# First block: high and low parts made from x times norm weight behind each residual sum, token norms applied to the products, embedding projection inside the FFN

## What is computed

```python
def rmsnorm(x, g):
    return x * lax.rsqrt(jnp.mean(x * x, axis=-1, keepdims=True) + EPS) * g

def first_block(...):
    h = x
    for i in range(2):
        hn = rmsnorm(h, norm_mix_g[i])
        if i == 0:  h = h + conv_dsa_mixer(hn, ...)        # stage "even"
        else:       h = h + gated_deltanet_mixer(hn, ...)  # stage "odd"
        # stage ffn0 / ffn1
        h = h + swiglu(rmsnorm(h, norm_ffn_g[i]), w_gate, w_up, w_down)
        # stage ple0 / ple1
        e = rmsnorm(p[i] @ ple_w_proj[i], ple_post_norm_g[i])
        h = h + e * jax.nn.sigmoid(rmsnorm(h, ple_norm_g[i]) @ ple_w_gate[i])
    return h
```

## Time and profile before

| | us |
|---|---|
| median of 3 runs (2429.23 to 2435.3) | 2432.1 |
| the profiled execution, whole | 2434.55 |
| its span, first to last instruction | 2433.2 |
| PE busy | 1919.7 (79%) |
| PE weight loads | 1371.9 (56%) |
| DVE busy | 949.6 (39%) |
| ACT busy | 709.6 (29%) |

### The profile page before, as it was taken

One profiled execution on the slowest core, in us unless ns is written; L12 is line 12 of the kernel. 1 busy time (PEld: TensorE's weight loads), 2 busy tenths in 40 slices (PEclk: granted clock), 3 DMA queues, 4 the chain that ended last, 5 costly groups with the idle time before them and its releaser, 6 DMA issues.

```text
span 2433.2 us, 30159 instructions
## 1 busy us (share of the span) xinstructions
PE 1919.7 (79%) x13222; PEld 1371.9 (56%) x13222; DVE 949.6 (39%) x1719; ACT 709.6 (29%) x1157; POOL 4.1 (0%) x11
## 2 busy tenths in 40 slices
PE   6788997788898998769877888978868765655656
PEld 4687997678776998637654333424246632322323
DVE  6765555666556554544463010101064520100001
ACT  4444444563524444334441000000034410000000
POOL 0000000000000000000000000000000000000000
PEclk9899998999999999889988999999988978888787
DMA  6234453331167545461042999999942369999997
GB/s 234 96 136 167 157 184 133 147 139 70 70 243 274 194 155 197 191 256 74 1 173 116 428 427 429 428 428 427 428 167 104 139 270 427 427 428 427 427 428 327
DMA packets 44787, 606.53 MB, mean 249 GB/s; under 512 B 5104, under 2 KB 5232, under 8 KB 6768
## 3 DMA queue, kind: packets, MB, share of 16 engines
q1 hardware_dynamic: 43488, 597.61, 60.8%
q0 software_dynamic: 880, 4.98, 0.6%
q10 hardware_dynamic: 288, 2.02, 0.2%
HBM read 603.54 MB, written 1.05 MB: 248 GB/s over the span
## 4 chain that ended last, share of the span: by engine, by line
PE 50%; DMA 28%; DVE 14%; ACT 6%; issue 2%; SPq 0%; DVEq 0%; POOLq 0%; ACTq 0%
PE ps L85 48%; DMA m_last_slot<-moe_down 15%; DMA m_more<-moe_up 9%; DVE m_WL L94 2%; PE ps L88 2%; ACT m_WH L91 1%; DMA m_ring<-ada 1%; ACT m_mix_sc L91 1%; DVE m_od L100 1%; DVE m_misc L103 1%; DVE m_wk L100 1%; DVE m_misc L112 1%; ACT m_od L91 1%; DVE m_wk L94 1%; DMA m_praw<-pT 1%
## 5 line engine op out<-in xcount | busy, mean ns | idle before, releaser
L85 PE MATMUL ps<-m_ring,m_moe_sc 128*32 128x256 f32 (+1 forms) x2304 | 414.8, 542 | 82.0 <-DMA m_ring<-moe_gate 76.9
L94 DVE TENSOR_TENSOR m_WL<-m_ring,m_WH 128x1024 fp32r<-128x1024 f32 (+1 forms) x277 | 331.8, 1203 | 310.7 <-ACT m_WH L91 310.3
L91 ACT ACTIVATE m_WH<-m_ring 128x1024 fp32r<-128x1024 f32 (+1 forms) x277 | 285.0, 1036 | 159.9 <-PE ps L85 153.1
L85 PE MATMUL ps<-m_nH,m_WH 128*128 128x256 f32 x1136 | 291.2, 292 | 14.9 <-ACT m_WH L91 14.8
L85 PE MATMUL ps<-m_nL,m_WH 128*128 128x256 f32 x1136 | 288.0, 289 | 3.0 <-DVE m_nL L94 3.0
L85 PEld LDWEIGHTS ps<-m_ring,m_moe_sc 128*32 128x32 f32 (+1 forms) x2304 | 155.8, 142 | 228.6 <-issue 115.9
L85 PE MATMUL ps<-m_more,m_moe_sc 128*32 128x256 f32 (+1 forms) x768 | 210.2, 562 | 85.3 <-DMA m_more<-moe_up 85.3
L85 PEld LDWEIGHTS ps<-m_nH,m_WH 128*128 128x128 f32 x1136 | 224.1, 197 | 20.9 <-ACT m_WH L91 17.3
L94 DVE TENSOR_TENSOR m_nT<-ps,m_nT 128x512 f32<-128x512 f32 (+1 forms) x32 | 17.9, 558 | 555.9 <-PE ps L85 555.9
L85 PEld LDWEIGHTS ps<-m_nL,m_WH 128*128 128x128 f32 x1136 | 224.0, 197 | 5.4 <-DVE m_nL L94 5.0
L91 ACT ACTIVATE m_nT<-ps 128x512 f32<-128x512 f32 (+1 forms) x64 | 31.4, 491 | 620.2 <-PE ps L88 327.2
(11 more groups left out here) (268 smaller groups left out, 2808.4 us busy)
## 6 DMA issues: line engine op xcount, KB each, us to landing
m_ring<-moe_gate SPq DMA_DIRECT2D x64, 2048.0 KB, 19.2
m_ring<-moe_up SPq DMA_DIRECT2D x32, 2048.0 KB, 17.7
m_more<-moe_up SPq DMA_DIRECT2D x32, 2048.0 KB, 22.2
m_more<-moe_down SPq DMA_DIRECT2D x32, 2048.0 KB, 18.0
m_last_slot<-moe_down SPq DMA_DIRECT2D x32, 2048.0 KB, 22.5
m_ring<-ada SPq DMA_DIRECT2D x24, 2048.0 KB, 8.2
m_ring<-ffn_down SPq DMA_DIRECT2D x16, 1408.0 KB, 6.1
m_ring<-ffn_gate SPq DMA_DIRECT2D x10, 2048.0 KB, 8.1
```

Of the source, the lines that this page charges most:

```text
L85: return Issued() if self.dry else self.e.matmul(out, lhsT, rhs, start=start, stop=stop, skip_group_check=skip)
L91: return Issued() if self.dry else self.e.activation(*a, **k)
L94: return Issued() if self.dry else self.e.tensor_tensor(*a)
```

## The change

- Parts of x: the next stage's high part is made by ACT as x times norm weight (a `[128,1]` scale of the activation) behind each residual sum, before that sum's square; the low part by DVE in one operation (x times weight minus high). No `rr` goes into them. `following(tag)` names the next stage. For odd they lie in new tiles `oddH`, `oddL`, and the tiles of odd are moved for it.
- The token norm `rr` is applied to products: DVE multiplies each gate tile pair by `rr` from PSUM to SBUF, and ACT takes Silu or Sigmoid there. `up` isn't scaled; the `down` sums are multiplied by `rr` before they are added to x. In even and odd, products with tokens on the partitions are scaled by ACT with `r_tok`, the others by DVE (`zc` by `rr2` = rr squared, one more multiplication of `z` before `zb`, q, k, v into `ou`).
- `pe_stats` comes behind the first unit of the stage (behind the product ki in even, ab in odd), with four more small matmuls for `r_tok` in even and odd.
- The embedding projection, its norm and the scaling of `er` move into the FFN: projection behind gate and up of tiles 4 to 7, its statistics behind tiles 8 to 11. POOL loads p after the mixer's last residual sum.
- Ada steps: one `fill(1)` each less at the start of ffn0, ffn1 and odd; `fill(2)` and `finish()` in ple, which the projection used, become one `fill(1)` that is an ada step.

```diff
+        def act_high(tag, outH, gain, k, n, ready):
+            act.wait_ge(*at(ready))
+            for q in range(k, k + n):
+                act.activation(outH(q), x8[:, q, :], ACT.Copy, scale=gain[:, q:q + 1]).then_inc(*A.mark(("nH", tag, q)))
+        def dve_low(tag, outH, outL, gain, k, n, ready):
+            dve.wait_ge(*at(ready))
+            for q in range(k, k + n):
+                dve.wait_ge(*at(("nH", tag, q)))
+                dve.scalar_tensor_tensor(outL(q), x8[:, q, :], gain[:, q:q + 1], outH(q).bitcast(F32), ALU.mult, ALU.subtract).then_inc(
+                    *V.mark(("nL", tag, q)))
...
+        def dve_after(tag, j):
...
+                dve_low(name, H, L, gain, j, 2, ("x", tag, j))
+            dve_square(tag, j, 2, 0)
+        def act_after(tag, j):
...
+                act_high(name, H, gain, j, 2, ("x", tag, j))
+            act_square(tag, x8, j, 2, 0, ("x", tag, j))
...
+                if room:
+                    r = room[j // 2 % 2].rearrange("p (k t) -> p k t", k=2)
+                    dve.wait_ge(*V.now()).tensor_tensor(r, part, by_r(2), ALU.mult).then_inc(*V.mark(("out", job, j)))
+                    dve.wait_ge(*V.now()).tensor_tensor(x8[:, j:j + n, :], x8[:, j:j + n, :], r, ALU.add).then_inc(*V.mark(("x", tag, j)))
...
                 if square:
-                    dve_square(tag, j - n, n, 0)
+                    dve_after(tag, j - 2)
...
         def pe_ffn(l, before):
-            pe_stats(tag, acc[0], [("ss", before, 0, 6)])
-            pe_jobs.fill(1)
...
+                if j0 == 0:
+                    next(gate)
+                    pe_stats(tag, acc[0], [("ss", before, 0, 6)])
+                run(gate)
+                run(pe_dense((tag, "up", j0), "ffn_up", (l,), js, 8, outH, outL, hr, lr, fg))
+                if j0 == 4:
+                    run(pe_dense((tag, "proj"), "ple_proj", (l,), list(range(8)), 2, lambda q: pH[:, q, :], lambda q: pL[:, q, :],
+                                 lambda q: ("pH", l), lambda q: ("pL", l), bg))
+                if j0 == 8:
+                    pe_stats((tag, "e"), wk[:, 0:512], [("sums", (tag, "e"))])
...
         def dve_ffn(l, before):
+                def gate(j, k):
+                    q = j0 + j
+                    dve.wait_ge(*at(((tag, "gate", j0), j))).wait_ge(*V.now())
+                    dve.tensor_tensor(f_sg[q // 2 % 2][:, 0:k * 256].rearrange("p (k t) -> p k t", k=k),
+                                      bank[(tag, "gate", j0), j][:, 0:k * 256].rearrange("p (k t) -> p k t", k=k), by_r(k), ALU.mult).then_inc(
+                        *V.mark(("gate scaled", l, q), ("out", (tag, "gate", j0), j)))
...
         def pe_ple(l):
-            pe_stats(tag, acc[0], [("ss", f"ffn{l}", 0, 6)])
-            pe_jobs.fill(2)
-            pe_jobs.finish()
...
             next(gate)
-            pe_stats((tag, "e"), wk[:, 0:512], [("sums", (tag, "e"))])
+            pe_stats(tag, acc[0], [("ss", f"ffn{l}", 0, 6)])
+            pe_jobs.fill(1)
             run(gate)
...
         def dve_ple(l):
             def gate(j, n):
+                dve.tensor_tensor(sv, bank[(tag, "gate"), j][:, :].rearrange("p (k t) -> p k t", k=2), by_r(2), ALU.mult).then_inc(
+                    *V.mark(("gate scaled", tag, j), ("out", (tag, "gate"), j)))
+                dve_after(tag, j - 2)
+                dve.wait_ge(*at(("gate", tag, j)))
                 dve.tensor_tensor(sv, sv, er[:, j:j + 2, :], ALU.mult).then_inc(*V.mark())
                 dve.wait_ge(*V.now()).tensor_tensor(x8[:, j:j + 2, :], x8[:, j:j + 2, :], sv, ALU.add).then_inc(*V.mark(("x", tag, j)))
-                dve_square(tag, j - 2, 2, 0)
...
         def pe_odd():
-            pe_stats("odd", acc[0], [("ss", "ple0", 0, 6)])
-            pe_jobs.fill(1)
-            run(pe_dense("ab", "od_in", (), [32], 8, outH, outL, hr, lr, fg))
+            run(pe_dense("ab", "od_in", (), [32], 8, oddH, oddL, hr, lr, fg))
+            pe_stats("odd", acc[0], [("ss", "ple0", 0, 6)], True)
...
         def dve_odd():
                         def take(j, n, dst=dst, w=w):
-                            dve.wait_ge(*at(("tap0", H, w, j + n - 1)))
+                            dve.wait_ge(*at((("qkv", H, w), j))).wait_ge(*V.now())
+                            dve.tensor_tensor(ou[:, j:j + n, 3:259], bank[("qkv", H, w), j][:, 0:n * 256].rearrange("p (k t) -> p k t", k=n), by_r(n),
+                                              ALU.mult).then_inc(*V.mark(("ou", H, w, j), ("out", ("qkv", H, w), j)))
+                            dve.wait_ge(*V.now()).wait_ge(*at(("tap0", H, w, j + n - 1)))
```

More of the change, by code:

```diff
@@ L707, in pe_even @@
             hr, lr = normed("even")
[L708 removed]
             run(pe_dense("ki", "ev_in", (), [28], 8, outH, outL, hr, lr, fg))
+            pe_stats("even", acc[0], ["first landed", ("ss", "start", 0, 6)], True)
             run(pe_tokens("qi", "ev_in", (), 24, yH, yL, both_t, hr, lr, fg))
@@ new lines, in act_ffn, with up @@
+        def act_ffn(l, before):
+            tag = f"ffn{l}"
+            A.begin(tag)
+            for j0 in range(0, 22, 4):
+                n_js = min(4, 22 - j0)
+                def gate(j, k):
+                    q = j0 + j
+                    s_ = f_sg[q // 2 % 2][:, 0:k * 256]
+                    act.wait_ge(*at(("gate scaled", l, q)))
+                    act.activation(s_, s_, ACT.Silu).then_inc(*A.mark(("ffn gate", l, q)))
+                def up(j, k):
+                    q = j0 + j
+                    act_parts(aH[:, q:q + k, :], f_at[q // 2 % 2][:, 0:k * 256].rearrange("p (k t) -> p k t", k=k), [("at", l, q)],
+                              *[("aH", l, i) for i in range(q, q + k)])
+                gates = act_dense(n_js, 8, gate)
+                if j0 == 0:
+                    next(gates)
+                    act_root(tag, rr)
+                run(gates)
+                run(act_dense(n_js, 8, up))
+                if j0 == 4:
+                    act_parts(pH, praw[:, :].rearrange("p (k t) -> p k t", k=2), [("p landed", l)], ("pH", l))
+                    run(act_dense(8, 2, lambda j, n: act_copy(er[:, j:j + n, :], bank[(tag, "proj"), j][:, 0:n * 256].rearrange("p (k t) -> p k t", k=n),
+                                                              [((tag, "proj"), j)], ("out", (tag, "proj"), j))))
+                    act.wait_ge(*A.now())
+                    act_sums((tag, "e"), er)
+                if j0 == 8:
+                    act_root((tag, "e"), r_e, [("sums", (tag, "e"))])
+            run(act_dense(8, 22, squares_of(tag)))
@@ L1127, in act_ple, with gate @@
             A.begin(tag)
+            def gate(j, n):
+                s_ = p_sg[j // 2 % 2]
+                act.wait_ge(*at(("gate scaled", tag, j)))
+                act.activation(s_, s_, ACT.Sigmoid).then_inc(*A.mark(("gate", tag, j)))
+                act_after(tag, j)
+            gates = act_dense(8, 8, gate)
+            next(gates)
+            act_root(tag, rr)
             if l:
@@ L1503, in dve_odd @@
             dve.wait_ge(*at("abT"))
-            dve.tensor_tensor(in2(g), gate[:, :, 0:8], both(sm("dt_bias")), ALU.add).then_inc(*V.mark())
-            dve.tensor_scalar(in2(a2), gate[:, :, 8:16], -1.0, None, ALU.mult).then_inc(*V.mark("ab read"))
+            dve.wait_ge(*V.now())
+            for t in range(2):
+                dve.scalar_tensor_tensor(g[:, 8 * t:8 * t + 8], gate[:, t, 0:8], r_tok[:, t:t + 1], sm("dt_bias"), ALU.mult, ALU.add).then_inc(*V.mark())
+                dve.tensor_scalar(a2[:, 8 * t:8 * t + 8], gate[:, t, 8:16], r_tok[:, t:t + 1], -1.0, ALU.mult, ALU.mult).then_inc(*V.mark("ab read"))
             dve.wait_ge(*V.now()).tensor_scalar(a1, g, -1.0, None, ALU.mult).then_inc(*V.mark())
```

297 lines of the change are left out of this document (140 added, 157 removed).

## The result

The changed kernel takes 2412.9 us (median of 4 runs, 2410.7 to 2416.0), the kernel before, run beside it, 2433.7 (2429.2 to 2436.5). The ratio is 0.9917, 95% interval 0.9897 to 0.9937. So the kernel is faster, as forecast, but by 20.8 us and not by 39.4. The time lies inside the range (2371 to 2414), at its slow end, and outside the bounds of the likeliest case (2383 to 2404). The profiled execution has a span of 2410.5 us at a mean granted clock of 0.916 (before: 2433.2 and 0.912), 22.7 less.

The account below looks back on a forecast made before the run. TensorE was taken as full inside FFNs, with time to win in waits between stages and ACT/DVE chains; gains and losses summed to 39.4 us, giving 2393 (likeliest case 2383 to 2404, chance 0.53), range 2371 to 2414.

Parts of the forecast that it names:

- Start: Start of the kernel, up to product qi: ki's end at 20, statistics to 22, then qi; gain 7 us.
- Even: Even mixer: four more DVE multiplications, two fewer ACT copies, partly on the path; loss 2 us, between 0 and 4.
- Even to ffn0 and odd to ffn1: Passages from mixer to FFN: the second gate unit starts earlier; gains 13 us and 4.5 us.
- FFNs: Both FFNs: projection, waits, statistics and a late low part cost 10.3 us each, loss 20.6; multiplying gates by rr costs nothing.
- ple0: First ple and start of odd, up to the cum matmuls: x pairs about 8 us apart, yet gain 26.5 us.
- Odd's projection: Pairs of odd's projection on the ACT and DVE chain take 8.0 us, was 6.74; six pairs, loss 7.5 us.
- jobs: Six more pairs of odd run among other work, at 0 to 1.3 us each; loss 3 us.
- ple1 and the tail: Second ple and ada chunks behind it: first streamed chunk lands at 39.8, last of eight at 74.8; gain 21.5 us.
- The first: Rival: DVE and ACT overlap, so chains in ple and odd are shorter; 2376 us, chance 0.19.
- The fourth: Rival: last slabs at ple and odd stay late because DVE is late, gain 12, not 26.5; 2407 us, chance 0.16.
- The second: Rival: TensorE falls to 1.2 GHz from waits in odd's projection and ple; 2426 us, chance 0.07.
- The third: Rival: the rr multiplication before Silu lengthens the FFN cycle, at 7.0 us giving 2447 us; chance 0.05.

Follow-up runs that it names:

- n1_noproj: The changed kernel without the embedding projection, its statistics and scalings in both FFNs, so ple adds nothing to x; 2387.4 us.
- e2_p: The changed kernel with high and low parts of p made ahead of the up product of tiles 4 to 7 in both FFNs; 2402.4 us.
- e3_scal: The changed kernel with the projection's eight scalings done two at a time behind gates of tiles 8, 12, 16 and 20; 2409.4 us.
- e1_c2: The changed kernel with c2's memset at the start of even and its Silu in ffn0, not in the first ada step; 2404.4 us.
- e6_ada: The changed kernel with c2 made early as in e1_c2, and four ada steps put in each FFN, eight in all; 2384.7 us.
- e4b_ple: The changed kernel with, in ple's gate, DVE's low parts behind the x sum and ACT's next unit's high part ahead of x's; 2408.3 us.
- e5b_odd: The changed kernel with, in odd's projection, DVE's rr multiplication ahead of low parts and ACT's Silu behind the next unit's high part; 2385.0 us.

## Why the prediction was right in sign and wrong in size

The waits and chains that the sum names are in the trace, and most of the gain came from them. What failed are sizes, in four steps above all, and one of these, in ple0, hides one-time work that the sum doesn't have: the first ada chunk in ple0 with the clock behind ffn0 (6.2 us), the start of the ada tail (4.0), the projection in the FFNs at full clock (3.9) and the length of a pair in odd's projection (3.2).

**Start, 5.3 for 7.** High and low parts came as worked out (the first matmul at 13.59, forecast 13 to 14). Two steps were too short. "ki's end at 20" came at 20.93, since the eight matmuls with the low weight part took 1.7, at the lower level of the clock. And "statistics (2.1 at half clock) to 22" left out the eight small matmuls by token, 1.6 at the same level: the statistics take 3.05, and qi starts at 23.98.

```profile
19.22 1.91 PE L85 MATMUL ps<-m_nH,m_WL 128*128 128x256 f32 x8
20.93 1.70 PE L85 MATMUL ps<-m_small,m_wk 128*128 128x1 f32 x8
22.49 2.05 PE L85 MATMUL ps<-m_wk,m_small 128*128 128x256 f32 x4
```

**Even, 0.4 for 2.** The term holds 1.0 that the start hands on: qi's first six matmuls take 2.41 us (23.98 to 26.39), before it was 1.37 (29.31 to 30.68). DVE's four more operations show no cost beside that. But even's length scatters by 4.6 us between executions in which it is the same, so this term can't be judged to better than that.

**Even to ffn0 and odd to ffn1: 13.5 for 13, 5.0 for 4.5.** Right in mechanism and size, the second with some luck: I read the second gate unit of before as starting at 771.9, but that is where the last slab's low part was used, and the unit starts at 773.07. The new unit was 0.5 later than worked out, which took back half of it.

**FFNs, 24.5 for 20.6.** The waits and the late low part were right (2.4 and 1.0 for 2.6 and 0.8). The step that failed: "the projection is 48 matmuls, 5.8", at full clock right behind a wait of 2 us. It had 1.4 more. The term should have been 12.2, which n1_noproj shows whole; e2_p shows 4.3 of it to be the wait and its clock, and e3_scal 1.3 to be the late low part, sized at 0.8. That `rr` on the gates costs nothing was right.

**ple0, 20.3 for 26.5.** This is the largest miss. The failed step is "the first gate unit ends at 5.1, statistics at 6.2, an ada chunk with its transposes 8.7". In the changed kernel the unit ends 5.8 us behind the FFN's last matmul, and the ada chunk starts at 10.6. I counted the step as if it were one of many. What I took out of the front of ffn0 (3.3 us "that comes back below") carried `c2` with it, and the new place had no cover for that: 4.5 of the 6.2, by e1_c2. The rest is the clock behind the FFN, which I had at full: ACT waits 2.28 us for the statistics here and 0.73 in e3_scal, where only the stretch's start and its clock differ. In e6_ada, with `c2` early and the clock at 1.00 there, the unit ends at 5.1 and the ada chunk starts at 6.1, as worked out, and the first sum of x comes 5.7 us sooner than in the changed kernel. The pairs were right (7.5 and 8.3 against 8 to 8.5), and the order "because they stand in DVE's queue before them" was the reason, by e4b_ple.

**Odd's projection, 10.7 for 7.5; jobs, 4.4 for 3.** The chain was right, its size was 0.36 a pair too small: "high parts of two units 1.9, low part 1.15" has both low parts in a row on DVE, 2.36, beginning 1.08 behind ACT's first. Six times 0.36 is 2.2 of the 3.2. Most of the rest stands at the start: the first multiplication comes 1.36 us behind `cum`, where the first copy of before came with it (469.30). For the jobs I had "0 to 1.3 each" without a row behind it; that they hang on the same chain was shown by e5b_odd, where its end gave 12.5 us among the mixes (2 us of that can be scatter).

**ple1 and the tail, 17.5 for 21.5.** The failed step is "the first lands at 39.8", with the end of ffn1 that it is compared with. Here 2.2 are a misreading. I took the group at 957.14 for ffn1's last matmuls and its start plus its time for the end, 958.25; in the trace of before DVE's last sum starts only at 960.54, so the last matmuls weren't in that row. The other part is that the first streamed chunk is used 42.5 us behind ffn1 and not 39.8, 2.7 late, of which 0.7 comes back behind the last chunk. No run was aimed at why it is late. Eight chunks at 4.9 were right.

**The rivals.** The first is refuted (the chains are as long as worked out). The fourth named a gain of only 12 in ple0. It had the right direction, but for another cause: the last slabs come late because the first sum does, 18.48 us behind the FFN, and not because of DVE. The second has a part: the clock was 0.80 in ple0 and 0.88 over odd's projection (0.78 from 457 to 480, in the middle of its pairs), so the sign that I had set, under 0.85, is there. Yet it follows the waits and doesn't set the pairs: the two orders changed in e4b_ple and e5b_odd brought the pairs to 6.4 and 5.7. The third is refuted by n1_noproj.

On the table load, the drain of about 1.38 us that the Trainium skill ("ScalarE: Activation LUTs", "What ACT_TABLE_LOAD costs") puts on top of a load isn't in this trace either: in ple0 a load starts at 387.23, 0.02 behind the end of the operation ahead of it, takes 1.28, and ACT's next operation begins 0.01 behind the load.

```profile
387.23 1.28 ACT L91 ACT_TABLE_LOAD   x1
388.52 0.20 ACT L91 ACTIVATE m_misc<-m_small 128x1 f32<-128x1 f32 x1
```

**Still open:** what makes even 174.5 to 179.1 us long and the second block 1421.2 to 1424.8 in executions with the same program there; what decides whether the clock falls behind an FFN; and why the medians of e1_c2 and e2_p gained more than their stretches (8.5 for 4.5, 10.4 for 8.5). The clock behind the FFNs is a part of that in the two profiled executions; whether it was so in the others isn't shown. No experiment was aimed at any of these.
